# Softmax normalisation in the attention turns: the multiply by the reciprocal of the sum moved from VectorE to ScalarE

## The reference

```
logits = einsum('bqhd,bkhd->bhqk', qi, k) * scale + c[t] - c[s]
logits = where(causal, logits, -inf)
probs  = softmax(logits, axis=-1)
out    = einsum('bhqk,bkhd->bqhd', probs, v)
```

## Time and profile before

| | |
|---|---|
| median of 3 runs | 648.5 us (648.17 to 648.59) |
| the profiled execution | 647.84 us, of which the span is 646.0 us |
| TensorE (PE) busy | 98% of the span |
| VectorE (DVE) busy | 60% |
| ScalarE (ACT) busy | 50% |
| GpSimd (POOL) busy | 48% |
| granted TensorE clock | 1.00 in all turns |

### The profile page before, as it was taken

The page is one execution under the profiler, slowest core; times in us unless marked ns, Lnnn a source line. Parts: engine busy times, 40 slices in busy tenths (PEclk is TensorE's granted clock), DMA queues, the critical chain, the costliest instruction groups (busy, mean ns, idle before and its releaser), DMA issues.

```text
span 646.0 us, 9283 instructions
## 1 busy us (share of the span) xinstructions
PE 632.9 (98%) x2932; PEld 517.4 (80%) x2932; DVE 388.1 (60%) x774; ACT 322.5 (50%) x557; POOL 308.2 (48%) x412
## 2 busy tenths in 40 slices
PE   8999999999999999999989999999999999999897
PEld 5788888888888888788767788888888887887686
DVE  5558678787878787455868635333434242456864
ACT  6748566565657575555665632321222122555451
POOL 1776554645545566000566558556544651001770
PEclk9999999999999999999999999999999999999999
DMA  6363334343334333153013223323222422350131
GB/s 203 109 203 109 107 106 134 116 110 111 116 112 127 125 106 107 33 195 131 2 60 104 97 74 122 117 78 130 74 94 92 129 99 97 97 164 32 33 131 65
DMA packets 27161, 68.69 MB, mean 106 GB/s; under 512 B 3568, under 2 KB 10096, under 8 KB 27136
## 3 DMA queue, kind: packets, MB, share of 16 engines
q1 hardware_dynamic: 27136, 68.37, 32.3%
HBM read 66.23 MB, written 2.13 MB: 106 GB/s over the span
## 4 chain that ended last, share of the span: by engine, by line
PE 90%; DVE 7%; ACT 2%; issue 1%; DMA 0%; SPq 0%; DVEq 0%
PE ps_pj L1031 25%; PE ps_pj L1033 25%; PE ps_pj L1032 25%; PE ps_tr L1040 3%; DVE act_lo L921 2%; PE ps_o L1142 2%; PE ps_o L1141 2%; PE ps_sc L1111 1%; DVE xT L917 1%; PE ps_sc L1109 1%; PE ps_tr L1031 1%; PE ps_tr L1033 1%; PE ps_tr L1032 1%; DVE t_a L926 1%; PE ps_o L1046 1%
## 5 line engine op out<-in xcount | busy, mean ns | idle before, releaser
L410 POOL TENSOR_TENSOR w_lo<-w_raw,w_hi 128x256 fp32r<-128x256 f32 x324 | 253.5, 816 | 127.4 <-ACT w_hi L470 117.9
L1031 PE MATMUL ps_pj<-act_hi,w_hi 128*128 128x512 f32 (+1 forms) x728 | 290.2, 399 | 5.4 <-DVE act_lo L921 4.3
L1033 PE MATMUL ps_pj<-act_hi,w_lo 128*128 128x512 f32 (+1 forms) x728 | 282.8, 389 | 0.0
L1032 PE MATMUL ps_pj<-act_lo,w_hi 128*128 128x512 f32 (+1 forms) x728 | 282.7, 388 | 0.0
L1031 PEld LDWEIGHTS ps_pj<-act_hi,w_hi 128*128 128x128 f32 x728 | 137.0, 188 | 36.5 <-DVE act_lo L921 7.9
L1033 PEld LDWEIGHTS ps_pj<-act_hi,w_lo 128*128 128x128 f32 x728 | 136.8, 188 | 28.7
L1032 PEld LDWEIGHTS ps_pj<-act_lo,w_hi 128*128 128x128 f32 x728 | 137.2, 188 | 24.5 <-issue 0.7
L470 ACT CAST w_hi<-w_raw 128x1024 fp32r<-128x1024 f32 x96 | 100.5, 1048 | 92.5 <-DMA w_raw<-in_weights 69.7
L445 POOL TENSOR_TENSOR acc<-acc,sq 128x512 f32<-128x512 f32 x14 | 21.3, 1525 | 115.4 <-ACT sq L618 114.6
L418 POOL TENSOR_TENSOR bias<-bias,future 128x128 f32<-128x128 f32 x64 | 32.1, 533 | 76.0 <-DMA bias<-negc_scratch 76.0
L525 ACT ACTIVATE logit<-logit,nmax 128x128 f32<-128x128 f32 (+1 forms) x64 | 36.0, 563 | 46.4 <-DVE nmax L766 46.0
(11 more groups left out here) (143 smaller groups left out, 741.4 us busy)
## 6 DMA issues: line engine op xcount, KB each, us to landing
w_raw<-in_weights SPq DMA_DIRECT2D x100, 512.0 KB, 3.4
bias<-negc_scratch SPq DMA_DIRECT2D x16, 256.0 KB, 7.4
bias<-negc_scratch SPq DMA_DIRECT2D x16, 192.0 KB, 6.2
xT<-in_xT SPq DMA_DIRECT2D x8, 256.0 KB, 4.4
bias<-negc_scratch SPq DMA_DIRECT2D x16, 128.0 KB, 4.8
out<-xT SPq DMA_DIRECT2D x7, 256.0 KB, 2.0
bias<-negc_scratch SPq DMA_DIRECT2D x16, 64.0 KB, 3.4
p_in<-in_pT SPq DMA_DIRECT2D x2, 512.0 KB, 4.6
```

What stands on the lines that cost most here:

```text
L410: last = nc.gpsimd.tensor_tensor(w_lo[place % RING][:, tiles], w_raw[stream(place) % RAW][:, tiles], w_hi[place % RING][:, tiles], ALU.sub ...
L1031: nc.tensor.matmul(out, w_h, a[0][:, k, tokens], start=k == first, stop=False)
L1032: nc.tensor.matmul(out, w_h, a[1][:, k, tokens], start=False, stop=False)
L1033: end = nc.tensor.matmul(out, w_l, a[0][:, k, tokens], start=False, stop=k == last)
```

## The change

`normalise` is split. VectorE keeps only the reciprocal, now called `sum_inverse`, and ScalarE gets the multiply, as an activation of kind Copy whose scale is the row's reciprocal. In ScalarE's order the multiply for block u stands in the group after its exponential, behind the exponential of block u+1. In VectorE's order the reciprocal of block u now stands ahead of `score_logits` of block u+1; before, it stood behind it.

```diff
+            def normalise(u, m0, jj):
+                b, n = u % LOGIT_BUFS, (u % TT + 1) * P
+                act.wait_ge(rec_done, count(u + 1 - 8, 8, m0, jj))
+                nc.scalar.activation(logit[b][:, 0:n], logit[b][:, 0:n], ACT.Copy, scale=rrec[:, b:b + 1]
+                                     ).then_inc(prob_ready, 1)
+
...
                     if attend and g in SCORE_AT:
                         score_exp(SCORE_AT[g], m0, jj)
+                    if attend and g - 1 in SCORE_AT:
+                        normalise(SCORE_AT[g - 1], m0, jj)
...
-            def normalise(u, m0, jj):
-                b, n = u % LOGIT_BUFS, (u % TT + 1) * P
+            def sum_inverse(u, m0, jj):
+                b = u % LOGIT_BUFS
                 dve.wait_ge(exp_done, count(u + 1 - 8, 8, m0, jj))
                 nc.vector.reciprocal(rrec[:, b:b + 1], rsum[:, b:b + 1]).then_inc(rec_done, 1)
-                dve.wait_ge(rec_done, count(u + 1 - 8, 8, m0, jj))
-                nc.vector.tensor_scalar(logit[b][:, 0:n], logit[b][:, 0:n], rrec[:, b:b + 1], None, ALU.mult
-                                        ).then_inc(prob_ready, 1)
...
+                    if attend and g - 1 in SCORE_AT:
+                        sum_inverse(SCORE_AT[g - 1], m0, jj)
                     if attend and g in SCORE_AT:
                         score_logits(SCORE_AT[g], m0, jj)
-                    if attend and g - 1 in SCORE_AT:
-                        normalise(SCORE_AT[g - 1], m0, jj)
```

## The result

| | before | with the change |
|---|---|---|
| median (4 runs each) | 648.34 us | 656.38 us |
| lowest to highest | 648.16 to 648.59 | 655.88 to 656.56 |
| ratio | 1 | 1.0122, 95% interval 1.0105 to 1.014 |
| the profiled execution | 647.84, span 646.0 | 655.88, span 654.1 |

The change makes the kernel 8.0 us slower. The forecast was 661.5, which rests on 13.2 us of added time, with a range of 653.5 to 667. The direction held; the size was 5 us too large.

The account below looks back on a forecast made before the run. TensorE was taken to bound turns 1 to 7, with waits only in the drain. Full turns 9.5 us plus drain 3.7 gave 13.2 on the profiled 647.84, 661.0; set against the median, 661.5 us, range 653.5 to 667.

Parts of the forecast that it names:

- Only the drain has waits to gain: Drain: three weight loads idle 0.56, 0.16 and 0.72 us before the change; in turns 1 to 7 nothing to gain.
- I take the middle, 1.35: Full turns, transposes of block 6: TensorE's load 1.65 us late, or about 1.05; 1.35 taken, 9.5 us over seven turns.
- the walk: Turn 6 followed instruction by instruction through blocks 4 to 6, to block 6 coming 1.65 us late.
- the string: VectorE and ScalarE: logits, exponential, reciprocal, next logits and next exponential each wait for the one before.
- the walk's quick case: Full turns: if the shifted first `q_lo` pair takes 1.39 us, block 6 is about 1.05 us late instead of 1.65.
- One thing can help: Full turn, VectorE: the first `q_lo` pair may take 1.39 us instead of 2.04, making all of this 0.65 earlier.
- Block 2 ... is just in time: Turn 6: block 2 multiplied by 196.97 us, against its weight load at 197.15.
- The weight roundings come under 1 us later: ScalarE's weight roundings: under 1 us later, each a group of four steps ahead of its use.
- ScalarE does not become the bound by its load. What counts is the order: Full turn: ScalarE's busy time rises from 18.67 to 22.4 of 29.8 us.
- faster: Rival: drain waits end with the moved work, so relieved VectorE gives back up to 1.4 us, 647.1; chance 0.04.
- The cover holds: Rival: TensorE never waits in turns 1 to 7 and only the drain pays 3.7 us, 652.2; chance 0.12.
- It compounds: Rival: scores wait for logits or block 2 misses its time; full turns lose 2.4 us, 669.5; chance 0.07.
- No difference: Rival: cover in all turns, drain included, 648.5 us; chance 0.05.

Follow-up runs that it names:

- The last experiment: Changed kernel with turn 1's weight rounding behind block 2's multiply, k_st roundings on VectorE, and the drain as before: 648.29 us, 1.0006 against the kernel before.
- experiment 56: Not a run number: The last experiment, in which 56 of the 64 multiplies are ScalarE's; 648.29 us, 1.0006 against the kernel before.
- the two halves: Against the kernel before: only the reciprocal moved ahead of the next logits, 648.78 us; only the multiply moved to ScalarE, 653.26 us.
- the kernel with the trimmed drain: Kernel before with, in the drain only, tanh and silu of z later and the half-output copy ahead of block 7's exponential: 647.32 us, 0.9994.

## Why the prediction was right, and where its sizes were off

1. **What bounds the kernel: right, but for 0.66 us.** Turns 1 to 7 are TensorE's, and VectorE's 3.8 us less per turn bought nothing. The last experiment shows it: without new stalls the time is that of before. "Only the drain has waits to gain" was not quite so: in turn 1 of the kernel before, two weight loads idle for 0.28 and 0.38 us.
2. **The drain: right in mechanism and size.** 3.7 us forecast, 3.36 measured; counted from the turn's start, the load of block 2 came 2.5 late, as forecast. Of it 0.9 is the reciprocal's new place (shown by moving it alone), and the first head gives about twice what the second does (1.95 and 1.0).
3. **The full turns: the stall at the right place, its size more than double.** "I take the middle, 1.35" was the step. The load of block 6 came 0.60 late, and a turn lost 0.42. Against the walk, in times from the turn's start: the splits and q copies came 0.66 late (forecast 0.83). The first `q_lo` pair took 1.37 us instead of 2.04, so the logits of block 4 were not late at all. The reciprocal ahead of the logits of block 5, priced at 0.19, was hidden. The distance from the logits of block 5 to those of block 6 was 1.35, forecast 1.32: this step of the string held.

   But the string did not make block 6 late against the kernel before. There the two logits stood 1.78 apart, and VectorE, relieved of the multiplies, now starts those of block 6 at 19.46 us of turn 6 instead of 19.92. What makes block 6 late is ScalarE's queue: its multiply stands behind the multiply of block 5, the k copies and the exponential of block 7, where VectorE's had a cover of 1.16. The string costs only against the kernel that keeps the reciprocal behind the next logits: there the load of block 6 stands at 23.62 us of turn 6, with the change at 24.00.

   From the walk's quick case, 1.05 (its terms, 1.65 less 0.65, give 1.00), take 0.17 and 0.19 and 0.64 to 0.69 is left; 0.60 was measured. That the turn loses less than the load (0.42 of 0.60) I put down to the load's running ahead of its matmul; that is argued, not shown.
4. **The case to take was the quick one.** "One thing can help" named it, and I took the middle for want of a reason. The trace of before had two: the pair takes 2.04 only in turns 4 to 7 and 1.37 to 1.52 in turns 1 to 3, and the slow pair overlaps GpSimd's work (last section). With the quick case the term would have been 7 x 1.05 = 7.4 and the forecast 659.6, still 3 us above the measured time. The recorded sum has a slip besides: 661.0 and 0.66 are 661.7, not 661.5.
5. **"Block 2 ... is just in time": right in turns 2 to 7, wrong in turn 1,** and "The weight roundings come under 1 us later" looked at their own users alone. In turn 1 the rounding waits 1.82 for its transfer with the multiply behind it. Turn 1 lost 1.60 of the 8 us; moving the rounding brought back 0.88 of it, moving the k copies 1.20, and with both turn 1 is as long as before (30.14 us). I had walked turn 6 and multiplied by seven. By the prediction's own sign, "if block 2 or the scores stall first", the walk is wrong for turn 1.
6. **"ScalarE does not become the bound by its load. What counts is the order": half right.** ScalarE is busy 22.00 of 30.20 us. But extra work that nobody waits for, at the same places in ScalarE's queue, cost 8.0 us too, at another wait of TensorE. Order and load can't be told apart where the queue has no gap. Taking 1.24 us out of the stretch mended the full turns, and so did taking away either head's multiplies or the reciprocal's new place (nearly): the loss begins where their sum exceeds the cover, and so the parts don't add up.
7. The rivals: *faster* fell, as the drain's first multiply-bound loads became later and not earlier. *The cover holds* (652.2) was nearer in size to the full turns' loss than 9.5 was, but it did not hold. *It compounds* has two conditions, and both occurred in one place each: block 2 missed its time in turn 1, and in the drain the scores waited 0.26 us for logits. No full turn lost 2.4. *No difference* fell with the 8.0.

The rule quoted in the prediction from the Trainium skill, "ScalarE: Activation LUTs", gives plain multiplies to VectorE; the outcome agrees with it. The 726 ns against 521 are not the reason here, though: in the last experiment 56 of the 64 multiplies are ScalarE's and cost nothing measurable.

## What to carry to other kernels

Before work goes to an engine with a low busy share, look for the stretch in which that engine's queue has no gap, and ask what stands at its end: there added work costs time as soon as the cover behind it is used up, however idle the engine is on average. Walk the first turn too, since a wait for a transfer that was harmless in a queue stops whatever is now put behind it. Where there is a cover, the cost of moved work is what exceeds it: parts tried one by one can each look nearly free and still cost together, as the two halves did in the full turns (0.00 and 0.1, together 0.42).

## What the hardware showed that I had not expected

- **The first `q_lo` pair of a turn takes 1.37 to 2.04 us, with GpSimd's work beside it or not.** Of the kernel before, timeline of GpSimd and VectorE, turn 1 and turn 4:

```profile
48.35 3.01 POOL L410 TENSOR_TENSOR w_lo<-w_raw,w_hi 128x256 fp32r<-128x256 f32 x4 [0.29 <-ACT w_hi L470]
...
51.65 1.37 DVE L827 TENSOR_TENSOR q_lo<-scaled,q_hi 64x512 fp32r<-64x512 f32 x2
...
137.68 3.46 POOL L410 TENSOR_TENSOR w_lo<-w_raw,w_hi 128x256 fp32r<-128x256 f32 x4
...
139.64 2.04 DVE L827 TENSOR_TENSOR q_lo<-scaled,q_hi 64x512 fp32r<-64x512 f32 x2
```

  In turn 1 GpSimd is done at 51.36 and the pair takes 1.37; in turn 4 they overlap by 1.5 us, and the pair takes 2.04 and GpSimd's four 3.46. With the change the same two in turn 6:

```profile
200.31 2.83 POOL L410 TENSOR_TENSOR w_lo<-w_raw,w_hi 128x256 fp32r<-128x256 f32 x4
...
203.75 1.37 DVE L832 TENSOR_TENSOR q_lo<-scaled,q_hi 64x512 fp32r<-64x512 f32 x2
```

  GpSimd ends at 203.14, the pair starts at 203.75, and it is so in all seven turns. Where GpSimd starts during a pair, as it does in the turn's second one, the pair keeps its 1.39. No run moved one of them alone, so this is a coincidence in time seen over 14 turns, and no more. Nor is it shown that the change makes the pair quick: in the kernel with the trimmed drain, whose turns are those of the kernel before, the pair takes 1.37 in five turns and 1.86 and 1.53 in turns 3 and 4, so the 2.04 that the prediction built on belongs to that one execution. The length of the overlap is no measure either, since those 1.86 overlap GpSimd by 0.62 only. The Trainium skill, "SBUF — State Buffer", section "SBUF: two separate sides", says that a VectorE operation with two SBUF inputs and a GpSimd operation that reads SBUF exclude each other for a whole instruction; by that rule the pair that misses GpSimd's work is the quick one, and the traces agree.

  What a slow pair costs can be read within one kernel. With only the multiply moved, the pair is slow in turn 4 alone, and there block 6 stalls for longer (0.20 to 0.27 in the other turns from 2 to 7) and the turn takes 30.27 us instead of 29.75 to 29.81:

```profile
142.70 1.82 DVE L832 TENSOR_TENSOR q_lo<-scaled,q_hi 64x512 fp32r<-64x512 f32 x2
...
152.56 0.31 PEld L1045 LDWEIGHTS ps_tr<-ident,logit 128*128 128x128 f32 x3 [0.71 <-ACT logit L531]
```

- **A Copy activation with a per-row scale takes about as long as an exponential here:** 726 ns against 724 on 512 columns, 387 against 402 on 128.
- **The granted clock stayed at 1.00** in turn 6 and in the drain, idle times of up to 1.6 us between weight loads included.
